# Two transformer blocks on one core: the gates' bias in three loads at later units, latent rows turned one product sooner, two splits of weights ahead of the merged rows' join

## The reference

```
h = rmsnorm(x, norm_g)
a_b,a_c,a_x,a_z, c_q,c_kv,k_pe,b_z, dq,dk,dv,c_z, gate_pre = split(h @ w_in)
y_a = a_b * conv(a_c * a_x) * silu(a_z)
q, k, v from rmsnorm(c_q) @ w_uq, rmsnorm(c_kv) @ w_ukv, k_pe   # 8 latent (MLA) heads of 96
y_b = causal_attention(rope(rmsnorm(q)), rope(rmsnorm(k)), v) * silu(b_z)
y_c = dilated_attention(rmsnorm(dq), rmsnorm(dk), dv; 3 groups, 8 heads) * silu(c_z)
g_a, g_b, g_c = split(sigmoid(gate_pre + b_gate), 3)
merged = g_a * (y_a @ w_out_a) + g_b * (y_b @ w_out_b) + g_c * (y_c @ w_out_c)
x = x + merged @ w_o
```

## Time and profile before

| | |
|---|---|
| runs | 1307.04, 1307.3, 1308.7 us; median 1307.3 |
| profiled execution | 1307.64 us, of which the profile's span is 1305.5 |
| PE busy | 1271.3 us (97% of the span) |
| DVE busy, ACT busy | 920.1 (70%), 781.0 (60%) |
| mean granted PE clock | 0.988 |
| DMA | 255.38 MB, 196 GB/s mean |

### The profile page before, as it was taken

The page is one execution under the profiler, slowest core; times in us unless marked ns, Lnnn a source line. Parts: engine busy times, 40 slices in busy tenths (PEclk is TensorE's granted clock), DMA queues, the critical chain, the costliest instruction groups (busy, mean ns, idle before and its releaser), DMA issues.

```text
span 1305.5 us, 17703 instructions
## 1 busy us (share of the span) xinstructions
PE 1271.3 (97%) x7012; PEld 1076.0 (82%) x7012; DVE 920.1 (70%) x1052; ACT 781.0 (60%) x1018; POOL 85.0 (7%) x77
## 2 busy tenths in 40 slices
PE   9999999999999999999999799999799998999997
PEld 7888888987788888888887799788688888998885
DVE  6576566687978755547785688857676947898574
ACT  7676545578646666646766665645368666656441
POOL 0000000000001000001351000000003510000000
PEclk9999999999999999999999899999899998999998
DMA  8676747534376866645879665766467796757562
GB/s 340 230 278 225 241 124 232 150 110 126 117 258 222 249 210 210 211 146 175 242 187 186 177 208 162 202 220 193 146 205 245 194 191 204 191 156 229 180 174 81
DMA packets 148419, 255.38 MB, mean 196 GB/s; under 512 B 91120, under 2 KB 91248, under 8 KB 148208
## 3 DMA queue, kind: packets, MB, share of 16 engines
q1 hardware_dynamic: 145520, 245.40, 62.7%
q10 hardware_dynamic: 2816, 8.84, 2.4%
HBM read 232.19 MB, written 1.05 MB: 179 GB/s over the span
## 4 chain that ended last, share of the span: by engine, by line
PE 75%; DVE 10%; DMA 6%; ACT 4%; issue 3%; POOL 1%; ACTq 0%; SPq 0%; another core or an unknown queue 0%; DVEq 0%; POOLq 0%
PE psum L2122 19%; PE psum L2143 18%; PE psum L2123 18%; PE psum L2128 5%; PE psum L2129 5%; PE psum L2175 5%; DMA swapped<-planes 4%; DMA raw<-weights 2%; PE psum L2321 2%; DVE w_lo L1326 2%; PE psum L2190 2%; DVE y_lo L1326 1%; ACT w_hi L691 1%; PE psum L2575 1%; DVE norm L1835 1%
## 5 line engine op out<-in xcount | busy, mean ns | idle before, releaser
L1326 DVE TENSOR_TENSOR w_lo<-raw,w_hi 128x1024 fp32r<-128x1024 f32 x220 | 267.1, 1222 | 136.7 <-ACT w_hi L691 135.4
L691 ACT ACTIVATE w_hi<-raw 128x1024 fp32r<-128x1024 f32 x220 | 229.9, 1054 | 134.6 <-PE psum L2143 75.8
L2122 PE MATMUL psum<-w_hi,x_hi 128*128 128x512 f32 x556 | 219.1, 394 | 0.3 <-ACT w_hi L691 0.3
L2123 PE MATMUL psum<-w_hi,x_lo 128*128 128x512 f32 x556 | 216.7, 390 | 0.0
L1326 DVE TENSOR_TENSOR y_lo<-raw,y_hi 128x1024 fp32r<-128x1024 f32 x138 | 167.6, 1221 | 53.5 <-ACT y_hi L691 52.4
L691 ACT ACTIVATE y_hi<-raw 128x1024 fp32r<-128x1024 f32 x138 | 144.5, 1053 | 47.4 <-PE psum L2143 19.9
L2143 PE MATMUL psum<-w_lo,x_hi 128*128 128x512 f32 x556 | 171.2, 389 | 0.0
L2122 PE MATMUL psum<-y_hi,x_hi 128*128 128x512 f32 (+1 forms) x372 | 146.5, 394 | 0.0
L2123 PE MATMUL psum<-y_hi,x_lo 128*128 128x512 f32 (+1 forms) x372 | 145.0, 390 | 0.0
L2122 PEld LDWEIGHTS psum<-w_hi,x_hi 128*128 128x128 f32 x556 | 104.9, 189 | 23.8 <-issue 2.3
L2143 PEld LDWEIGHTS psum<-w_lo,x_hi 128*128 128x128 f32 x556 | 104.7, 188 | 22.0 <-DVE w_lo L1326 0.4
(11 more groups left out here) (232 smaller groups left out, 2329.1 us busy)
## 6 DMA issues: line engine op xcount, KB each, us to landing
raw<-weights SPq DMA_DIRECT2D x406, 512.0 KB, 4.3
probs<-weights SPq DMA_DIRECT2D x8, 512.0 KB, 5.5
probs_t<-weights SPq DMA_DIRECT2D x8, 512.0 KB, 5.6
arena<-gains ACTq DMA_DIRECT2D x7, 512.0 KB, 4.7
arena<-gate_bias ACTq DMA_DIRECT2D x2, 1536.0 KB, 22.4
norm<-x_feat SPq DMA_DIRECT2D x4, 256.0 KB, 4.9
res<-x SPq DMA_DIRECT2D x2, 512.0 KB, 7.7
arena<-lru_w ACTq DMA_DIRECT2D x1, 1024.0 KB, 4.8
```

Source lines behind the costliest of these rows:

```text
L691: act.activation(slot(t)[0], raw_place(t), ACT.Copy).then_inc(hi_ready, 1)
L1326: dve.tensor_tensor(lo, raw_place(t), hi.bitcast(F32), ALU.subtract).then_inc(lo_ready, 1)
L2122: pe.matmul(out_, l_hi, r_hi, start=start, stop=False, skip_group_check=skip)
L2123: pe.matmul(out_, l_lo, r_hi, start=False, stop=False, skip_group_check=skip)
```

## The change

Four edits, all in the two layers:

1. The bias is loaded in three DMAs of 512 KB, gate m at c = 11 + m, behind `refill(t + 1)` and ahead of `exps` in ACT's order; DVE waits for all three at c = 17.
2. `turn_mla(0)` and `turn_mla(1)` go behind the last product of chunk 7 instead of the first of chunk 8.
3. At c = 8, ACT's copies of the turned rows 0 and 1 go from behind `refill(t + 1)` to ahead of the copy of chunk 7's values, and those of rows 2 and 3 from behind `refill(t + 3)` to right behind `dil_pack(5)`, ahead of `refill(t + 2)`.
4. On DVE the refills for t and t + 1 stand whole ahead of `merged_join()`. Before, one tile (103) was ahead of it; tiles 104 and 105 came behind `add_product(4)`.

```diff
@@ ACT, loop over c @@
                     if c > 1:
                         refill(t)
+                    if c == 8:
+                        for r in range(2):
+                            act.wait_ge(mla_turned, At(r + 1, l, 4))
+                            act.activation(mla_t[0:QK, 4 * r:4 * r + 4, :].rearrange("p h s -> p (h s)"),
...
-                    if c == 9:
-                        act.dma_start(ga_t[:, :, 0, :], gate_bias[l, :, :].rearrange("p (m n) -> p m n", n=D)
-                                      ).then_inc(bias_loaded, 16)
...
                     refill(t + 1)
+                    if 7 <= c <= 9:
+                        key_gain(c - 4)
+                    if 4 <= c <= 8:
+                        dil_pack(c - 3)
                     if c == 8:
-                        for r in range(2):
+                        for r in range(2, 4):
                             act.wait_ge(mla_turned, At(r + 1, l, 4))
...
-                    if 7 <= c <= 9:
-                        key_gain(c - 4)
-                    if 4 <= c <= 8:
-                        dil_pack(c - 3)
...
+                    if 11 <= c <= 13:
+                        m = c - 11
+                        act.dma_start(ga_t[:, m, 0, :], gate_bias[l, :, m * D:(m + 1) * D]).then_inc(bias_loaded, 16)
                     if 0 <= u < UNITS_LAYER:
                         exps(At(UB + u + 1, l, UNITS_LAYER), rows2[u])
                     refill(t + 2)
                     refill(t + 3)
...
-                    if c == 8:
-                        for r in range(2, 4):
-                            act.wait_ge(mla_turned, At(r + 1, l, 4))
...
@@ DVE, c = 17 to 22 @@
-                        dve.wait_ge(bias_loaded, At(16, l, 16))
+                        dve.wait_ge(bias_loaded, At(48, l, 48))
@@ DVE, end of a layer @@
                 add_product(3)
-                refill(t, 1)
+                refill(t)
+                refill(t + 1)
                 merged_join()
                 bank_rests(x_lo, x_hi, 0, probs_t, 0.5, merged_hi, At(4, l, 4), merged_lo)
                 dve.wait_ge(weights_used, t + 2)
                 add_product(4)
-                refill(t + 1)
                 refill(t + 2)
                 refill(t + 3)
@@ PE, behind product q of chunk c @@
-                        if c == 8 and q == 0:
+                        if c == 7 and q == 3:
                             pe.wait_ge(mla_ready, At(1, l, 1))
                             pe.wait_ge(up_copied, At(2, l, 2))
                             turn_mla(0)
                             turn_mla(1)
```

More of the change, by code:

```diff
@@ L1171, in _ @@
                         refill(t)
+                    if c == 8:
+                        for r in range(2):
+                            act.wait_ge(mla_turned, At(r + 1, l, 4))
+                            act.activation(mla_t[0:QK, 4 * r:4 * r + 4, :].rearrange("p h s -> p (h s)"),
+                                           wide((6, 4)[r % 2], 1024)[0:QK, :], ACT.Copy,
+                                           scale=lp[0:QK, L_GCOL + r // 2:L_GCOL + r // 2 + 1]
+                                           ).then_inc(mla_copied, 1)
                     if c == 3:
```

## The result

The runs of after lie at 1275.38 to 1277.53 us with a median of 1276.47, those of before beside them at 1302.36 to 1308.7 with a median of 1307.17: a ratio of 0.977, interval 0.9745 to 0.9798. The change is faster by 30.7 us. The forecast was 1274.5 in a range of 1272 to 1283. The profiled execution of after took 1275.38 us, of which 1273.2 are span, so it is the shortest of the four.

The account below looks back on a forecast made before the run. PE works almost throughout, so only its waits and low clock move the end. Bias 18.2, turns 2.9 and splits 12.0 sum to 33.1 us; 1307.6 - 33.1 = 1274.5, range 1272 to 1283.

Parts of the forecast that it names:

- Bias, 18.2: Scores of unit 1, both layers: moving the bias removes 12.3 us of waits and 3.3 + 2.6 of low clock.
- What is late next: At the scores of unit 1, once the bias is moved: nothing that the trace shows is late next.
- its bound of 2.7 to 5.2 us: Delay that one 512 KB part of the bias can cost a unit's transpose: from 0 over 2.7 to 5.2 us.
- The cover of 6.9: Between DVE's join of unit 1 and its reader on PE, 6.9 us of delay are hidden; 0 to 5.2 fits inside.
- Turns, 2.9: Latent rows turned one product sooner, copies moved on ACT: waits of 2.0 and 0.9 us go, from 2 to 3.
- Splits, 12.0: Two splits ahead of the merged join: add_product(5) starts 4.8 and 3.8 us sooner, plus 1.6 and 1.8 of clock.
- the four large ones: PE's main wait reasons: merged turn 12.7 us, scores of unit 1 12.3, second latent turns 2.0, scores of unit 0 0.9.
- The first rival, the clock: The clock falls all the same at the shortened merged-turn waits: 1.6 to 3.3 us per layer, say 1279; chance 0.25.
- the row at 1.31 us: A PE wait of 1.31 us in 690:700, before sixteen turns, left the clock at 1.00; taken as guide for 2.0.
- only the splits move: End of layers: tile 108's load or split is late again, each layer keeps 2.3 us, 1278.5 or 1282; chance 0.06.
- the bias is not what held job 5: Job 5's transpose is slow because of weights queued with it; parts two and three alone, 1292.7; chance 0.04.
- The slower one: Each of six bias parts delays a unit's transpose by 17.7 us, 82 us in all, 1356; chance 0.03.

Follow-up runs that it names:

- the eleven matmuls: The kernel after with eleven matmuls of 128x512, results overwritten, ahead of the merged turn in each layer: 1274.19 us, ratio 0.9765.
- everything but the bias: The kernel after with the bias put back as one load of 1536 KB at c = 9 on ACT's queue: 1300.68 us, ratio 0.9954.

## Why the prediction was right, step by step

**Bias, 18.2.** Right in place and size: alone it gave 19.5. The transpose landed in 4.9 against 5.8, and the join came at 710.51 against 709.8. "What is late next" held: nothing. But the reason in the change's form was half idle: the cut into three, with its bound of 2.7 to 5.2 us for each transpose, did not matter. The unit transposes beside the parts took 5.8, 5.5 and 7.2 us in layer 0 against 3.8 before, that is 1.7 to 3.4 more, inside the bound (at the second place it was 5.5 also in the kernel with the load on SP's queue, where no part is near, so not all of it comes from the parts), and 3.7 to 3.8 in layer 1. The cover of 6.9 hid them: DVE's joins at 738.36 and 752.30 did not wait and that at 765.67 waited 0.38. One thing was left out: the cover ahead of the scores of unit 1 was to be 7.7, or 5.7 behind two splits, and was 5.1, because PE itself comes sooner once its waits ahead of this place are gone (719.35 against 729.34 - 8.06 = 721.28).

**Turns, 2.9.** Right, on a condition that the text did not state. The turns started at 688.81 against a forecast of 688.2 and waited for nothing, and the copies' waits (2.9) are gone from the list. Alone the part gave nothing, since it stands ahead of a place where PE waits for something else. In a sum of parts each is priced with the others made; here that was said for none of them.

**Splits, 12.0.** The mechanism was right, a term was too large. From join to `add_product(5)` it took 9.2 us; the prediction has 14.0 - 4.8 = 9.2. Tile 108 held nothing up. In sum the two waits were to fall by 8.6 and fell by 7.3. The waits left were to be 2.1 and 2.0, and were 2.67 and 2.70. The missing 1.3 is PE's own arrival. I kept it where it was (930.73 - 6.87 = 923.9, that is 9.2 us behind the join), but in before PE had also waited for a low part on the way there. PE in before, 905:925, shows it:

```profile
921.75 0.73 PE L2143 MATMUL psum<-y_lo,x_hi 128*128 128x512 f32 x2 [0.45 <-DVE y_lo L1326]
```

With tiles 104 and 105 split early this wait of 0.45 goes too (0.22 in layer 1), and PE arrives 912.64 - 2.67 - 901.47 = 8.5 us behind the join, 0.7 sooner; 0.2 of that has no row. It then waits so much longer for a DVE that comes when it did. Waits that vanish ahead of a wait which is bound by another engine are no gain; I had left this small one out because it is not among the four large ones.

**The first rival, the clock.** It held in part. In the profiled execution layer 0 lost 3.06 x 0.47 = 1.4 us and layer 1 nothing; the mean clock of the other runs, 0.997 or 0.999, and the 3.0 us which the eleven matmuls gave, suggest that one layer loses it or both; only the profiled execution shows where. The prediction took nothing, since 2.0 is nearer to the row at 1.31 us than to the one at 4.2. This is the term that was mis-sized. The rows of after now stand at 2.67, with half the clock, and 2.70, without. The Trainium skill (TensorE: Matmul & The Clock Gate, Part 4: PE-mode transpose) had been cited for this rival, because eight transposes follow the wait. By that rule both layers should have fallen, since both have the same eight; the trace agrees in one of two. With matmuls ahead of the turns instead of a wait, the same eight transposes follow and the clock stays, so transposes alone do not bring it down.

**The account.** Forecast for the profiled execution 33.1, measured 32.3: 1.3 lost at the two longer waits and 1.4 at the clock of layer 0, which leaves some 1.9 gained beyond the sum. Small waits that are gone from the list hold 1.0 of it (0.7 and 0.3 in before's list, on L1326 and L691); the rest lies in PE's busy time, which fell by 8.9 where the clock explains 9.3 - 1.4 = 7.9 (a new wait of 0.2 takes a little of it back). No row tells why. The median is 1.1 above the profiled execution. The clock is part of that: the two runs with a mean of 0.997 took 1276.7 and 1277.5, the two with 0.999 took 1275.4 and 1276.2.

There is luck in how near the numbers are. The prediction took 0.2% for what a measurement of this kernel can tell, from three runs; the kernel before then spread over 1296.1 to 1313.7 in one batch, 1.3%. All terms were read off one of its executions, in which layer 1's wait was 4.2 us; in another kernel with the bias at c = 9 it was 10.1, in a third it was absent. After does not spread like this, so its 1276 doesn't hang on luck, but the size of the gain does.

**The other rivals.** That only the splits move is out: ACT waited 4.22 us at tile 110, behind the place that counts. That the bias is not what held job 5 is out by the kernels with the bias alone and with everything but the bias. The slower one is out by the whole load at c = 11.

**Left open.** Why the transpose beside the bias takes 12 to 23 us at c = 9 and the units' transposes 3.6 to 7.4 at c = 10 to 13. Two things differ at once: at c = 9 loads of weights are in flight when the transpose and the bias start, at c = 10 and 11 SP had paused; and at c = 9 the bias is issued 0.2 to 0.7 us behind the transpose, elsewhere 1.3 behind or 4.4 ahead. No run was made to take these apart. The weights alone don't do it: with them and no bias the transposes ahead of job 5's took 5.8 in the median. One place in after bears on it, where the third part of the bias follows unit 3's transpose; the two issues and the landing of the transpose:

```profile
758.42 4.28 SPq L602 DMA_TRANSPOSE swapped<-planes  x1
...
758.50 0.35 ACTq L1255 DMA_DIRECT2D arena<-gate_bias  x1
...
swapped<-planes SPq DMA_TRANSPOSE x1, 7.2
```

The part comes 0.08 us behind the transpose, and SP had issued nothing for 5.7 us (its last issue ended at 752.75). The transpose took 7.2 us. So a load close behind on the other queue is not enough either, and the weights in flight are the likelier condition; that this part has a third of the bytes is not ruled out.

The eleven matmuls were not tried together with the whole load at c = 11, which would be the version to try next. The fastest that ran is the one with the eleven matmuls, by 2.3 us of median against after and 1.4 against the load on SP's queue, each in another batch.

## What to carry to other kernels

Look in the DMA view for a transpose on the path that is far above the median of its kind (here 21.5 us against 5.8), and for what the second queue carries then. Here it helped to move that load to a later time or to put it on the same queue behind the transpose, and cutting it did not help. A kernel whose time spreads far more than that of its relatives is worth this look too. Price the parts of a change in the order in which the waits stand; a gain ahead of a wait that another engine sets is none, and a wait that remains can be dearer in clock than in time, so work in its place may pay. When splits or copies are reordered, follow the raw place that each one frees to the load that waits for it, and to what stands behind that load in order on the engine: this is where the order with `add_product(5)` ahead of the splits lost more than it won.

## What the runs showed of the hardware

- **Two queues at once, one with a transpose.** In before, the stretch 704:725 moved 129 GB/s while the mean share of the 16 DMA engines was 1.13, that is full. In the kernel with the whole load at c = 11, the stretch 733:743 moved 358 GB/s at 1.06.

```profile
704.00:725.00 21.00, 16.80 (x91) 14.24 (x90) 3.59 (x3) 7.83 (x9) 0.00 (x0) 1.00 1.13 129
```

```profile
733.00:743.00 10.00, 10.00 (x85) 9.34 (x85) 9.39 (x9) 4.89 (x11) 0.00 (x0) 1.00 1.06 358
```

  The engines are taken in both, and in the first they move a third of it. In the lines of queues shown with the experiments (packets, MB, share of 16 engines), those of the kernel with everything but the bias, 704:725, the 2372 packets of q1 hold the engines for 81.7% of 21 us and carry 1.61 MB; at c = 11, 733:743, 2475 packets carry 2.00 MB in 60.1% of 10 us. So nearly as many packets held the engines (0.817 x 21) / (0.601 x 10) = 2.9 times as long. The Trainium skill (DMA: Bandwidth & Descriptors, Queues, rings and completion order) says that each DMA engine takes turns between the queues it has work for, a packet at a time. By that the transpose loses at most the time of the bias's own packets. As an estimate from the rows above, these held the engines for 0.461 x 10 = 4.6 us at c = 11. The 6.9 us at c = 10 against 3.8 agree with it; 21.5 against 4.9, which is 16.6 more, do not.
- **The collision varies.** At c = 9 the one load of the bias on ACT's queue landed in 14.3 to 25.3 us, and the transpose beside it in 12.1 to 22.9. That this is what spreads those kernels' times (4 to 18 us, against 1 to 4 without it) is likely, but only the profiled executions show the landings.
- **A wait of 2.7 us and the clock.** The same wait, with the same instructions behind it, left the clock at 1.00 in one layer and at about half in the other.

```profile
1251.11 1.26 PE L2190 MATMUL psum<-cst,arena 128*128 128x128 f32 x8 [2.70 <-DVE arena L1893]
```

  In the kernel with the whole load at c = 11 it was the other way round, 1.00 in 908:917 and 0.83 in 1246:1256, and in that with the load at c = 10 as well (1.00, and 0.82 in 1247:1256). No run shows what decides it.
- **DMA issues ahead of their engine's arithmetic.** In after the first part of the bias was issued from ACT's queue at 732.80, in the middle of the activation (L1220) that ACT began at 732.56, that took 1.02 us and that stands ahead of it in the order.
